# Own signal for the first norm vector, later compression weights, other places for a gate tile's digits, tail started with token tile 0

## What is computed

```python
h = rmsnorm(x, norm_mix[i])
z = h @ w_in[i]                       # 1024 x 5400
y_a = nsa_mixer(...z...) @ w_up_nsa[i]   # compressed, selected and window attention
y_b = retention(...z...) @ w_up_ret[i]
x = x + (sigmoid(merge_a) * y_a + sigmoid(merge_b) * y_b) @ w_out[i]
h = rmsnorm(x, norm_mlp[i])
x = x + square(relu(h @ w_ff1[i])) @ w_ff2[i]
gate = sigmoid(rmsnorm(x, norm_ple[i]) @ w_ple_gate[i])
x = x + gate * (p[i] @ w_ple[i])
```

## Time and profile before

| | us |
|---|---|
| median of 3 runs | 1510.5 |
| lowest, highest | 1509.44, 1510.59 |
| profiled execution | 1510.71 |
| its span | 1508.8 |
| PE busy | 1456.8 (97%) |
| DVE, ACT, POOL busy | 784.9, 715.9, 286.6 |
| mean granted clock of PE | 0.993 |

### The profile page before, as it was taken

How to read it: one execution, slowest core, us unless ns; L and a number is a source line. 1 busy time by engine, 2 the same in 40 slices (tenths; PEclk the granted TensorE clock), 3 DMA queues, 4 the chain that set the end, 5 groups by cost and what they waited for, 6 DMA issues and landing times.

```text
span 1508.8 us, 19744 instructions
## 1 busy us (share of the span) xinstructions
PE 1456.8 (97%) x8540; PEld 1221.2 (81%) x8540; DVE 784.9 (52%) x993; ACT 715.9 (47%) x901; POOL 286.6 (19%) x109
## 2 busy tenths in 40 slices
PE   5999999999999999999999999999999999999998
PEld 4787868989867787679899778687989888889986
DVE  3336445544562455355445569885444457554445
ACT  4465425445445463436454436655455326255452
POOL 3689140000026595320000000000000004000000
PEclk9999999999999999999999999999999999999999
DMA  9632435645538432435555373405555453056451
GB/s 352 230 113 91 163 112 188 231 168 198 194 112 290 155 124 87 167 132 215 184 196 195 112 217 112 140 13 204 202 182 208 144 188 120 31 201 237 175 181 70
DMA packets 123142, 250.25 MB, mean 166 GB/s; under 512 B 16960, under 2 KB 28976, under 8 KB 122928
## 3 DMA queue, kind: packets, MB, share of 16 engines
q1 hardware_dynamic: 122792, 248.89, 46.6%
q10 hardware_dynamic: 264, 0.10, 0.0%
HBM read 247.93 MB, written 1.05 MB: 165 GB/s over the span
## 4 chain that ended last, share of the span: by engine, by line
PE 87%; DVE 5%; SPq 3%; ACT 2%; DMA 2%; issue 1%; DVEq 0%; ACTq 0%
PE psum L457 84%; PE psum L464 3%; SPq L2931 2%; DMA ring<-in_w_in 2%; DVE work L1312 1%; DVE x L2445 1%; DVE w_lo L1051 1%; SPq L2956 0%; SPq L2927 0%; DVE rows L1312 0%; ACT w_hi_work L1031 0%; ACT w_hi_tmp L1031 0%; ACT w_hi_rows L1031 0%; DVE ht_hi L1285 0%; DVE tiny L2488 0%
## 5 line engine op out<-in xcount | busy, mean ns | idle before, releaser
L457 PE MATMUL psum<-ht_hi,w_lo 128*128 128x256 f32 x960 | 270.3, 282 | 4.5 <-DVE ht_lo L1312 2.9
L457 PE MATMUL psum<-w_lo,ht_hi 128*128 128x512 f32 (+1 forms) x576 | 225.4, 391 | 0.0
L457 PE MATMUL psum<-w_lo,hid_hi 128*128 128x512 f32 x512 | 202.5, 395 | 0.0
L457 PEld LDWEIGHTS psum<-ht_hi,w_lo 128*128 128x128 f32 x960 | 180.6, 188 | 6.9 <-issue 5.9
L1031 ACT ACTIVATE w_hi_work<-ring 128x2048 fp32r<-128x2048 f32 x43 | 82.3, 1914 | 186.7 <-PE psum L457 170.7
L1051 DVE TENSOR_TENSOR w_lo<-ring,w_hi_work 128x2048 fp32r<-128x2048 f32 x31 | 71.1, 2293 | 137.6 <-ACT w_hi_work L1031 137.6
L457 PEld LDWEIGHTS psum<-w_lo,ht_hi 128*128 128x128 f32 x576 | 109.3, 190 | 21.1 <-issue 1.0
L1121 DVE TENSOR_TENSOR hid_lo<-work,hid_hi 128x512 fp32r<-128x512 f32 x60 | 41.5, 692 | 162.0 <-ACT hid_hi L1099 162.0
L457 PE MATMUL psum<-ht_lo,w_hi_rows 128*128 128x256 f32 x448 | 125.1, 279 | 0.0
L457 PE MATMUL psum<-ht_lo,w_hi_tmp 128*128 128x256 f32 x448 | 125.1, 279 | 0.0
L457 PE MATMUL psum<-ht_hi,w_hi_tmp 128*128 128x256 f32 x448 | 125.0, 279 | 0.0
(11 more groups left out here) (371 smaller groups left out, 3303.4 us busy)
## 6 DMA issues: line engine op xcount, KB each, us to landing
ring<-in_w_ff SPq DMA_DIRECT2D x32, 2048.0 KB, 7.9
ring<-in_mlp_w SPq DMA_DIRECT2D x32, 2048.0 KB, 8.5
ring<-in_w_in SPq DMA_DIRECT2D x20, 2048.0 KB, 8.1
ring<-in_w_out SPq DMA_DIRECT2D x4, 2048.0 KB, 8.1
ring<-in_w_ple_gate SPq DMA_DIRECT2D x4, 2048.0 KB, 8.2
ring<-in_sb_ssm_w_in SPq DMA_DIRECT2D x4, 2048.0 KB, 11.5
ring<-in_dsa_w_in SPq DMA_DIRECT2D x3, 2048.0 KB, 8.1
ring<-in_w_up_nsa SPq DMA_DIRECT2D x2, 2048.0 KB, 7.9
```

The source lines that it names most:

```text
L457: ins = pe.matmul(o, lhsT, rhs, start=start, stop=stop)
```

## The change

Four edits:

1. norm_mix gets a signal `mix_in` of its own; the other eight share `small_in`. In layer 0 `turn_small` waits for norm_mix alone and turns 8 rows; after the four x pieces PE waits for the other eight and turns all 64 rows again into a score bank, and DVE, behind piece 3, copies columns 8 to 63 (a wait on `cols_ready`, a copy, a wait on `cols_saved`). In layer 1 both signals are waited for at once. POOL's wait for the constants moves from its start to just before the rotary embedding.
2. In SP's order w1, w2 and p of each layer come behind in3's load, ahead of in4's wait. The constants stay ahead of in3.
3. gate0's high digits go to `tab0` and `big`. gate1 keeps its places. No tile takes `work` behind ff2.6. DVE subtracts the first half of gate0 ahead of the x updates and the second half after the second update (n == 1), ahead of the first token's split.
4. The tail's PE multiplies groups q = 0 and 1 of sb3 for token tile 0 alone: q = 0 before `turn_x(2)`, q = 1 between it and `turn_x(3)`. Behind the turns of C come the second token tile of q = 0 and 1, and all of q = 2 and 3. There are 16 more products, because the 32 products of q = 0 and 1 have 128 columns each where 16 had 256.

```diff
@@ -155,6 +155,7 @@
             "in4": ("hT", "work"), "in5": ("z0", "big"), "in6": ("scr", "zb"), "in7": ("work", "hT"),
             "in8": ("zb", "scr"), "in9": ("work", "hT"), "in10": ("zb", "hT"),
             "out0": ("work", "zb"), "out1": ("mid", "tmp"),
+            "gate0": ("tab0", "big"), "gate1": ("tmp", "rows"),
             "dso0": ("big", "big_a"), "dso1": ("big_b", "work")}
     first = {"ff1.0": ("scr", "z"), "A.ff1.0": ("scr", "z"), "B.ff1.0": ("scr", "b4a")}
     turn = [name for name in splits if name not in late]
@@ -378,7 +379,7 @@
 
 
     const_in, ident_in, x_in = sig("const_in"), sig("ident_in"), sig("x_in")
-    small_in = sig("small_in", 16 * 9)
+    small_in = sig("small_in", 16 * 8)
     late_in = sig("late_in", 16 * 3)
     w1_in, ple_in = sig("w1_in", 16 * len(W1_PARTS)), sig("ple_in", 16)
     small_used = sig("small_used", 1, 1)
@@ -405,6 +406,7 @@
     out_ready, out_saved = sig("out_ready", 4), sig("out_saved", 4)
     ple_ready, ple_added = sig("ple_ready", 4), sig("ple_added", 4)
     x_high = sig("x_high", 4)
+    mix_in, cols_ready, cols_saved = sig("mix_in", 16), sig("cols_ready"), sig("cols_saved")
 
     ht_split, ht_high = sig("ht_split", 12), sig("ht_high", 4)
     turned, gained = sig("turned", 4), sig("gained", 4)
@@ -707,10 +709,13 @@
     def turn_small(head):
 
         pe, st = head.pe, head.st
-        pe.wait_ge(small_in.sem, st.at(small_in, 16 * 9))
+        n = 64 if st.where.layer else 8
+        pe.wait_ge(mix_in.sem, st.at(mix_in, 16))
+        if st.where.layer:
+            pe.wait_ge(small_in.sem, st.at(small_in, 16 * 8))
         b, nth = head.aux.next("cols")
         pe.wait_ge(head.aux.saved.sem, st.at(head.aux.saved, nth))
-        head.kit.mm(b[:, 0:64], vec_rows, ident[0:64, 0:64], True, True, head.aux.ready)
+        head.kit.mm(b[:, 0:n], vec_rows[0:n], ident[0:n, 0:n], True, True, head.aux.ready)
 
     def layer_head(pe, st):
         return Head(pe, st, (WIDE, AUX), (TILES, SPLITS, PLACES), turn_small, [f"n{n}" for n in range(4)])
@@ -780,6 +785,8 @@
         if st.where.layer == 0:
             for n in range(4):
                 head.turn_x(n)
+            pe.wait_ge(small_in.sem, 16 * 8)
+            pe.matmul(scores[:, 0:64], vec_rows, ident[0:64, 0:64], start=True, stop=True).then_inc(cols_ready.sem, 1)
             chunk(0)
         else:
             chunk(0, None, {(0, 2): lambda: head.turn_x(2), (0, 5): lambda: head.turn_x(3)})
@@ -1290,7 +1297,8 @@
 
         b, nth = head.aux.next("cols")
         head.dve.wait_ge(head.aux.ready.sem, head.st.at(head.aux.ready, nth))
-        head.dve.tensor_copy(cols, b[:, 0:64]).then_inc(head.st.up(head.aux.saved), 1)
+        n = 64 if head.st.where.layer else 8
+        head.dve.tensor_copy(cols[:, 0:n], b[:, 0:n]).then_inc(head.st.up(head.aux.saved), 1)
         head.dve.wait_ge(head.st.last.sem, head.st.reached())
 
     def save_plain(head, b, n):
@@ -1367,6 +1375,9 @@
             for h in range(2):
                 lower_half(st, dve, TILES, SPLITS, "in0", h)
             head.turned(3)
+            dve.wait_ge(cols_ready.sem, 1)
+            copy(cols[:, 8:64], scores[:, 8:64]).then_inc(cols_saved.sem, 1)
+            dve.wait_ge(cols_saved.sem, 1)
         else:
             head.turned(2)
             head.turned(3)
@@ -1581,7 +1592,7 @@
         low(2)
         low(3)
         dve_mlp(st, dve, "", TILES, SPLITS)
-        lower_split(st, dve, TILES, SPLITS, "gate0")
+        lower_half(st, dve, TILES, SPLITS, "gate0", 0)
         dve.wait_ge(norm_ready.sem, st.at(norm_ready, 1))
         for n in range(4):
             t, c = divmod(n, 2)
@@ -1589,6 +1600,8 @@
             xv = x[:, t, c * BANK:(c + 1) * BANK]
             dve.scalar_tensor_tensor(out=xv, in0=scores[:, n * BANK:(n + 1) * BANK], scalar=nrr[:, t:t + 1], in1=xv,
                                      op0=ALU.mult, op1=ALU.add).then_inc(st.up(ff2_saved), 1)
+            if n == 1:
+                lower_half(st, dve, TILES, SPLITS, "gate0", 1)
             if n % 2:
                 split_turned([f"np{n - 1}", f"np{n}"], C_PLE, t)
         lower_split(st, dve, TILES, SPLITS, "gate1")
@@ -1619,6 +1632,7 @@
 
         chunks = wide.again(WIDE)
         pool.wait_ge(chunks.saved.sem, st.at(chunks.saved, chunks.nth_save("c4t1")))
+        pool.wait_ge(const_in.sem, 16)
         t4 = [tmp[:, n * 512:(n + 1) * 512].rearrange("p (t h d) -> p t h d", t=TT, d=64) for n in range(4)]
         cos, sin = (bc(K[n].rearrange("p (t d) -> p t d", t=TT), 2, RH) for n in ("cos", "sin"))
         for a, col in enumerate((Z_RQ, Z_RK)):
@@ -1877,7 +1891,17 @@
                 mm(o, ca4[:, j, :], states[:, 0, j, :], False, False)
                 mm(o, ca4[:, SJ + j, :], states[:, 1, j, :], False, True, aux_.ready if j % 8 == 7 else None)
 
+        pe.wait_ge(aux_.saved.sem, st.at(aux_.saved, aux_.nth_save("A.x1")))
+        w = next_tile("sb3", KT, BANK)
+
+        def state_input(q, tok):
+            for k in range(KT):
+                mm(scores[:, q * S + tok.start:q * S + tok.stop], w[:, k, q * P:(q + 1) * P], hT[:, k, tok], k == 0, k == KT - 1,
+                   u_ready if q == 3 and k == KT - 1 else None)
+
+        state_input(0, slice(0, P))
         head.turn_x(2)
+        state_input(1, slice(0, P))
         head.turn_x(3)
         pe.wait_ge(c_in.sem, st.at(c_in, 64))
         for ri in range(2):
@@ -1887,11 +1911,10 @@
                 tp(b[:, i * P:(i + 1) * P], cin[:, ri, i].rearrange("p u n -> p (u n)"),
                    signal=aux_.ready if i == 3 else None)
         pe.wait_ge(aux_.saved.sem, st.at(aux_.saved, aux_.nth_save("A.x3")))
-        w = next_tile("sb3", KT, BANK)
-        for q in range(4):
-            for k in range(KT):
-                mm(scores[:, q * S:(q + 1) * S], w[:, k, q * P:(q + 1) * P], hT[:, k, :], k == 0, k == KT - 1,
-                   u_ready if q == 3 and k == KT - 1 else None)
+        for q in range(2):
+            state_input(q, slice(P, S))
+        for q in range(2, 4):
+            state_input(q, slice(0, S))
         tile_done()
         w = next_tile("sb0", KT, BANK)
         kit.units_by_tile(wide_, ["sq0", "sq1"], w)
@@ -2920,12 +2943,12 @@
                 sp.wait_ge(small_used.sem, i * small_used.per_layer + 1)
             small = small_loads(i)
             if i:
-                for dst, s in small[:9]:
-                    sp.dma_start(dst, s).then_inc(small_in.sem, 16)
+                for n, (dst, s) in enumerate(small[:9]):
+                    sp.dma_start(dst, s).then_inc((small_in if n else mix_in).sem, 16)
             for n, name in enumerate(TILES):
                 if n == RING and i == 0:
                     sp.dma_start(const[:, P:CONST_W], I["const"][:, P:CONST_W]).then_inc(const_in.sem, 16)
-                if n == RING:
+                if n == RING + 1:
                     for kind, j0, nj, place in W1_PARTS:
                         s = src("cmp_w1_" + "kv"[kind])[j0 * P:(j0 + nj) * P, :]
                         sp.dma_start(place.rearrange("p (j n) -> p j n", n=CMP_HID),
@@ -2975,8 +2998,8 @@
         act.sem_inc(wide.saved.sem, 2)
         act.dma_start(ident, I["const"][:, 0:P]).then_inc(ident_in.sem, 16)
         act.wait_ge(small_used.sem, 1)
-        for dst, s in small_loads(0)[:9]:
-            act.dma_start(dst, s).then_inc(small_in.sem, 16)
+        for n, (dst, s) in enumerate(small_loads(0)[:9]):
+            act.dma_start(dst, s).then_inc((small_in if n else mix_in).sem, 16)
         act.wait_ge(eps_set.sem, 4)
         act.wait_ge(x_in.sem, 16)
         steps = [Steps(Where(i)) for i in range(DEPTH)] + [None]
@@ -3004,7 +3027,6 @@
 
     @block.gpsimd
     def _(pool):
-        pool.wait_ge(const_in.sem, 16)
         for i in range(DEPTH):
             st = Steps(Where(i))
             if i == 0:
```

## The result

| | before | after |
|---|---|---|
| median, us (4 runs each) | 1509.97 | 1517.59 |
| lowest, highest | 1507.53, 1510.59 | 1516.94, 1520.16 |
| profiled execution, its span | 1510.71, 1508.8 | 1517.17, 1515.4 |
| mean granted clock of PE in it | 0.993 | 0.990 |

The ratio is 1.0061, 95% interval 1.0047 to 1.0074: 7 to 11 us slower, clear of noise. The forecast was 1513.3 with a range up to 1517.0; the time lies 0.6 above that range. So the sign of the sum was right, and its size was not.

What follows compares the result with a forecast made beforehand. TensorE (PE), 87% of the chain that ended last, was taken as the bound. Won 10.75 and lost 13.5 us, net 2.8 slower than the profiled 1510.71, gave 1513.5; the median 0.2 below, 1513.3; 80% range 1504.5 to 1517.

Steps and rivals of the forecast that it cites:

- Step 1: At the start, PE waits for norm_mix alone; second token begins at 24.5 against 27.68: 3.2 us won.
- The collision with the fourth piece of x: At the start, DVE's split of that piece may wait for POOL's first 4.6 us; without it 3.8 us won.
- Step 2: Weights load later: chunk 2 wins 4.0 us in layer 1, 0.3 in layer 0; chunk 3 stalls lose 5.4 per layer.
- R + 27.3: in4's landing, 27.3 us after in0's slot is released at the end of chunk 1's first product, when in3 is issued.
- Step 3: gate0's digits moved at each layer's end: x updated earlier, PE's wait before x transposes gone, 1.15 us won per layer.
- step 4: Layer 1's in0 split earlier, POOL clear of DVE's cast: PE's 2.03 us wait goes, 2.1 us won.
- Step 5: Tail's head: moved products wait for sb3 and the turned C comes later for DVE: 2.7 us lost.
- The term for sb3: In the tail, PE reaches the moved products before sb3 lands at 889.5 and idles 3 us, where before 1.8.
- The wait before the second score batch: In the tail, the later turned C delays DVE's softplus, so PE waits 2 to 2.5 us more.
- A: in4 isn't held up, so both new chunk 3 stalls go: 8.0 us faster, 1502.5; chance 0.15.
- B: At the start norm_mix lands no sooner than the other vectors, nothing won: 1516.5; chance 0.10, shared with larger stalls.
- C: The tail keeps its gain, sb3 in time or DVE's delay absorbed: -0.7 to +1.1, sum 1510.5; chance 0.17.

Runs made afterwards that it cites:

- tail_only: The kernel before, with only the tail's early sb3 products moved ahead of the turns of C: ratio 1.0071 to before, 1515.4 us without the pause.
- w1 in halves: w1 of keys behind in3, the other weights behind in4: 1499.56 us with the norm_mix and gate0 edits, 1505.80 alone in the kernel before.
- no_tail: The changed kernel with all sb3 products put back behind the turns of C: ratio 0.9981 to before, 1509.1 us without the pause.
- weights_only: The kernel before, with only w1, w2 and p loaded behind in3: ratio 1.0061 to before, 1517.2 us without the pause.

## Why the prediction was wrong

**Step 1 (forecast 3.2 won).** At the start 4.05 were won: 15.93 against 19.98. norm_mix landed by 6.34, not 6.9. The comparison takes in luck: the profile of the kernel before started late. PE's first 512-column product begins at 18.74 to 19.98 in the five traces with the old start, at 15.93 to 16.43 in the nine with edit 1; the means are 3.1 apart. The collision with the fourth piece of x did not come, because POOL waits for that split before in1 (its idle time ends with it, [19.42 <-DVE ht_lo]); I had read POOL's start from ACT's digits alone. A collision came just behind that piece, where nothing waited for it. DVE's two small copies there took 0.41 us before and now:

```profile
19.94 9.15 DVE L1326 COPY tiny<-work 64x64 f32<-64x64 f32 x2
```

They end at 29.09, as POOL's two halves of in1 do (19.86 to 29.04). My bound of 3.8 without a collision was a slip: 19.98 - 16.5 is 3.5. The number fits, but the runs showed that the gain isn't kept without edit 2. That is a dependence that the sum, which added the steps, did not hold: edit 1 alone loses 3.6. In the changed kernel the gain lasts: its first 512-column product comes at 15.93 and the second token of chunk 3 at 61.58; with edit 2 alone the two come at 18.86 and 64.92.

**Step 2 (4.3 won, 10.8 lost).** Both halves were there. Layer 1's stall of 2.15 went and nothing stands in its place in chunk 2. ACT's split of in4 in layer 0, and its release 27.65 us after in3's issue at 29.59, where R + 27.3 was forecast:

```profile
57.24 1.91 ACT L1038 ACTIVATE w_hi_hT<-ring 128x2048 fp32r<-128x2048 f32 x1 [10.43 <-DMA ring<-in_w_in]
59.06 1.89 ACT L1038 ACTIVATE w_hi_work<-ring 128x2048 fp32r<-128x2048 f32 x1
```

The idle times were 3.88 and 3.14 against a forecast 3.5, and 4.26 and 3.34 in the second profiled execution. The fall behind them came in layer 0, and in layer 1 not: at 496 to 500 the clock is 1.00, so that stall cost 3.1 and not 5.4. In the second profiled execution both fell, layer 0 twice. The four stalls with their falls cost 5.6, 3.1, 7.7 and 5.0 us, 5.4 in the mean, so this step holds. The Trainium skill, DMA: Bandwidth & Descriptors, on queues, rings and completion order, has descriptors taken in ring order; in4's landing behind w1 agrees.

**Step 3 (1.15 each) and step 4 (2.1).** These held. Edit 3, which brings both, measured 4.7 against 4.4. POOL's work on in0 ended at 443.51 (forecast near 441, and before 442 as the sign), because ACT's split for it began at 430.86, not near 429, and its first half took 6.10 us. That is still ahead of DVE's cast, which took 0.43 instead of 3.12:

```profile
432.84 6.10 POOL L1058 TENSOR_TENSOR w_lo<-ring,w_hi_work 128x2048 fp32r<-128x2048 f32 x1 [216.66 <-ACT w_hi_work L1038]
438.90 4.61 POOL L1058 TENSOR_TENSOR w_lo<-ring,w_hi_zb 128x2048 fp32r<-128x2048 f32 x1
...
447.94 0.43 DVE L1292 CAST ht_hi<-hT 128x512 fp32r<-128x512 f32 x1
```

Up to the end of gate1 the steps give 3.2 + 4.3 - 10.8 + 2.3 + 2.1 = 1.1 us won. Measured: 4.5; of the 3.4 between, 2.1 are the stalls, above all the fall that did not come in layer 1, and 0.85 the start; the last 0.5 weren't traced.

**Step 5 is the one that failed: 3.85 us lost (2.7 with layer 1's 1.15) was forecast from gate1's end on, and 11.1 were.** Both waits that it named were there and larger than forecast, and the falls of the clock behind them, which are the largest part of the miss, it had put at nothing. The term for sb3 was 3 us of idle. SP's queue in the tail, before and then after (start, length, line, load):

```profile
844.17 0.58 SPq L1766 DMA_DIRECT2D p_sb<-in_ssm_lam_re  x1
...
868.12 6.77 SPq L1759 DMA_DIRECT2D big<-in_ssm_b_im  x1
...
878.72 9.64 SPq L1797 DMA_DIRECT2D ring<-in_sb_ssm_w_in  x3
```

```profile
841.05 0.58 SPq L1780 DMA_DIRECT2D p_sb<-in_ssm_lam_re  x1
...
863.90 8.59 SPq L1773 DMA_DIRECT2D big<-in_ssm_b_im  x1
...
876.95 12.81 SPq L1811 DMA_DIRECT2D ring<-in_sb_ssm_w_in  x3
```

From the first small load to sb3's issue it took 34.55 us before and 35.90 after; from there to the landing 10.8 before, and to PE's start 11.65 after. PE was ready 42.34 us behind the first small load, as forecast (886.55 - 844.17 = 42.38). 3.0 + 1.35 + 0.85 is 5.2, which is what was measured: I had taken SP's and the landing's times from one trace as constants. With 0.35 before C that is 5.56 against the 1.80 before: 3.76 more, forecast 1.2. C was turned at 897.41, where I had forecast 897.5, and that is chance: the whole tail stood 3.1 us earlier (the first small load at 841.05 instead of 844.17), so against the rest of the tail C came 3 us later than forecast.

The wait before the second score batch was 2.88 (forecast 2 to 2.5). I had built it from a late C: 5 us late, 1.7 absorbed. The runs show it as a property of the order instead: 2.9 with two calls ahead of C whether sb3 is late or early, 1.40 with one, no wait with none.

And beside the one fall that the kernel before has there too, nothing in the step was set aside for the clock. The windows show one fall more at 887 to 895, one at 962 to 966 and one at 1303 to 1308, 1.7 us each, and the second profiled execution has the same three. The idle times, 3.76, 2.88 and 0.35 more at 1302, less some small ones that shrank, are the 6.7 by which PE's idle time grew. The three falls are 5.1; 0.6 of that passed while PE stood still before 888.60 (the granted clock was 0.69 at 887 to 888 and 0.50 at 888 to 889), so 4.5 should show as busy time, and 4.3 do. Together that is the 11.1.

The last of the three may not be edit 4's. The wait at that place is 0.98 to 1.00 us in all nine traces with edit 1 and 0.63 in all five without it, tail_only's among them; a fall followed in five of the nine and in none of the five. Why edit 1 lengthens a wait 1300 us later is open.

**Luck.** The errors had opposite signs: up to gate1's end the change did 3.4 us better than forecast, behind it 7.2 worse. That the time lies only 0.6 above the range is owed to the first. With steps 1 to 4 as forecast it would have been near 1521.

**The rivals.** A (no stall) is what w1 in halves made true, not the change. B was wrong: norm_mix landed early, at 6.34 to 6.87 in the eight traces that show it. C was the opposite of what came. The point from which the forecast should have been wider is the clock: I gave a new fall a price (1.9; measured 1.7) only behind the stalls of step 2, and the range up to 1517.0 left no room for three more.

## What to carry to other kernels

Before a step is moved ahead of another on a busy engine, ask two things: can its input's queue deliver it then (here SP had 36 us of small loads in front), and who starts from the step that is pushed back. A gain ahead of a transfer whose time is set by the queue's bytes since the launch, like in3's at 46 us, is no gain until the transfer moves; cost such edits together, not one by one. And a new wait is dearer than its length: beside 2.9 us of idle stands the chance of a fall of the clock at 1.7 us each.

## What was not expected of the hardware

The price of a fall was 1.70 or 1.71 us at every place in all fourteen traces (or a whole multiple of it in a longer stretch), the end of the span left out; whether it came didn't follow the wait: none after 3.14 us (496.39) or after 2.92 (947.22), one after 1.47 (237.79) in one layer and not in the other, one after 0.98 (1302.32). Two executions of one kernel differ by that, and profiles of single executions say little on differences under 3 us.

The pause of 15 us on the first chip is DVE kept waiting by POOL. DVE, then POOL, in the trace of edits 1 and 3:

```profile
123.92 12.20 DVE L1320 TENSOR_TENSOR work<-work,tiny 128x512 f32<-128x512 f32 x1
```

```profile
125.46 4.62 POOL L1058 TENSOR_TENSOR w_lo<-ring,w_hi_scr 128x2048 fp32r<-128x2048 f32 x1
130.04 5.53 POOL L1643 TENSOR_TENSOR tmp<-big,const 128x256 f32<-128x256 f32 x8
135.65 1.05 POOL L1646 TENSOR_TENSOR big<-tmp 128x256 f32<-128x256 f32 x1
```

In the profile of before the same operation takes 2.07 us: it begins at 120.92 beside POOL, waits for POOL's next change of instruction, at 122.36, and ends 0.6 us behind it. Here it lasts over POOL's changes at 125.46 and 130.04 and over those between the eight short ones behind, and ends at 136.12. Two small ones behind it took 4.47 and 4.13 us, beside two of POOL's of 4.5 each, and PE stood still for 15.04. The two other profiled executions with the pause (no_tail, weights_only) have the same 12.20 and 15.04. The Trainium skill, SBUF — State Buffer, on two separate sides, says that whoever starts first of a VectorE operation with two SBUF inputs and a GpSimd one holds the shared ports for its whole instruction. The trace agrees that DVE is shut out, not slowed; that DVE may be passed over again and again while POOL's instructions follow each other without a gap is what these rows add. By their times (over 1520) 11 of before's executions on that chip held it and 3 to 8 of the twelve of each variant; no profile of the other chips shows it. What decides it wasn't tried.
